# Attention on pairs of heads: wide turnings, scores in two row halves, values stationary, weights divided before the product

## The chip, the cores and the metric
One core of one Trainium2 chip. The metric is the device time of one execution in microseconds (us). All data are fp32; a product written in fp32 is issued on TensorE as two passes, and the large projections are split by hand into a high and a low part in fp32r.

## The reference, cut to what matters
Two layers, each a token mixer of three branches and a mixture of experts, over 128 context tokens (stream 0) and 128 latent tokens (stream 1). The change is in branch A, attention with 8 heads of 64 columns:

```
q, k, v = heads of proj columns; scale = 64 ** -0.5
context:  p = softmax(q k^T * scale);                 o = p v
latent:   q, k = axial_rope(q), axial_rope(k)
          s = [q k^T * scale + bias + window mask , q k_ctx^T * scale]
          p = softmax(s);                             o = p[:, :128] v + p[:, 128:] v_ctx
y_att = all heads' o side by side (128 x 512)
merged = gate0 * (y_att @ w_branch[0]) + gate1 * (y_ssm @ w_branch[1]) + gate2 * (y_gm @ w_branch[2])
```

## The kernel before, in words
The program is written out by hand for the five engines, and each runs its instructions in the order in which they stand; semaphores join them. In the mixer every weight piece (`PIECES`, 1 MB each) is loaded by SyncE's queue into one of four slots, its high part `wh` is made by ScalarE (`convert_to`, L1550) and its low part `wl` by VectorE (L1859), in three rotating parts; `ahead(key)` makes all pieces up to two behind `key`. TensorE then makes three groups of products for a piece. GpSimd's queue loads the rows for the modulation (`adaw`), sixteen slices in a layer, in two buffers.

The attention stage has four units in the order (stream s, head group g) = (0,0), (0,1), (1,0), (1,1), four heads each. TensorE's order in a unit: turn q and k of the unit (`turn4`, at s=1 also the cached keys `kctx`), a filler piece (`fill(FILL[3 * i])`), a modulation slice (`accumulate`), the scores, a second filler, two slices, turn S (`pw`, at s=1 also `pc`), a third filler, a slice, the product with v (at s=1 also with `vctx`) into bank `o`. In unit (1,0) it also turns `dtrow` and the modulation row `ada_row` ahead of the scores. After the four units it turns the rows of the branch, `branch_rows(l, 0, q)`, and after one more filler makes the branch's product.

VectorE's order in a unit: copy the turned q, k (and cached keys) to `qT`, `kT`, `cTk`; convert ahead; at i=2 the `dt` rows (`dtx`) and the modulation; read the scores: maximum and subtraction (s=0), or bias, window, copy, maximum, subtraction (s=1); after unit (0,1)'s scores the convolution of two blocks (`convolve`, `filled(3)`); convert ahead; then wait for `prob` and make the row sums of S (L2247) and their reciprocal (L2249); convert ahead; and last read bank `o`, multiplied by the reciprocal, into q. ScalarE makes the exponential of S (L1691, `prob`), copies the turned S to `pT` (L1698), and makes the activations of the fillers.

Banks 5, 6 and 7 are given out in turn to the small products (`odd` in `make_plan`); `bank_free` and `bank_emptied` wait until the last user of the bank has read it. `keep_busy` issues products whose result nobody reads.

## Time and profile before
| what | us |
|---|---|
| median of 3 runs | 1217.45 (1212.9 to 1221.46) |
| the profiled execution, its own time | 1216.07 |
| its span, first to last instruction | 1214.3 |
| TensorE busy | 1136.5 (94%) |
| VectorE busy | 634.9 (52%) |
| ScalarE busy | 442.4 (36%) |

The span is what the trace covers; the execution's own time has 1.8 us more around it. In the trace the attention stage of layer 0 lies from 78 to 181 us, that of layer 1 from 660 to 769 us. A busy share is a mean over the whole program; what counts for the change is, in these stretches, which engine is waited for at each hand-over.

### The profile page before, as it was taken

The page shows a single profiled execution, that of the slowest core. Times are in us where ns is not written, and L with a number is a line of the kernel's source. Part 1 is how long each engine was busy: PE and PEld are TensorE (multiplying, and loading weights), DVE is VectorE, ACT ScalarE, POOL GpSimd, SP SyncE. Part 2 cuts the span into 40 slices and gives each one's busy share as a digit, 9 for nine tenths or more (in the row PEclk, how much of TensorE's full clock was granted, in tenths as well). Part 3 has the DMA queues.
Part 4 walks back from the last instruction along what each step waited for, and adds up shares of the span by engine and source line. Part 5 has one row for each costly group of instructions (what it writes and reads, how often), then busy time and mean ns, then how long its engine had stood idle before and what let it go on. Part 6 is the DMA issues. An engine that isn't in the chain of part 4 may idle for free.

```text
span 1214.3 us, 18618 instructions
## 1 busy us (share of the span) xinstructions
PE 1136.5 (94%) x7288; PEld 787.3 (65%) x7288; DVE 634.9 (52%) x1298; ACT 442.4 (36%) x742; POOL 67.0 (6%) x113
## 2 busy tenths in 40 slices
PE   4999999999989999999979999999998989999994
PEld 0777777887766556666557776878776656666652
DVE  0645667788554533332278374679865453333224
ACT  0634553554332222222263344635533222222222
POOL 0401000101000000000020000010000000000000
PEclk8899999999999999999989989999998999999997
DMA  9997864546999999999667866556476999999960
GB/s 352 303 330 265 302 243 161 175 147 223 381 410 410 408 409 409 409 408 398 223 183 237 307 246 243 174 172 217 144 275 251 374 406 386 407 398 404 401 235 36
DMA packets 107981, 360.06 MB, mean 297 GB/s; under 512 B 9220, under 2 KB 12768, under 8 KB 99696
## 3 DMA queue, kind: packets, MB, share of 16 engines
q1 hardware_dynamic: 97392, 301.41, 66.0%
q0 software_dynamic: 10496, 57.39, 13.6%
q8 instruction: 61, 1.00, 0.3%
q14 instruction: 32, 0.26, 0.1%
HBM read 356.06 MB, written 3.74 MB: 296 GB/s over the span
## 4 chain that ended last, share of the span: by engine, by line
PE 68%; DVE 14%; DMA 5%; ACT 5%; issue 4%; DVEq 3%; ACTq 1%; SPq 0%
PE bank L920 63%; PE bank L923 5%; DVE wl L1859 3%; ACT wh L1550 2%; DMA adaw<-in_w_ada 2%; DMA first<-in_w_ada 2%; DMA raw<-in_w_in 1%; DVE merged L1859 1%; DVEq L2206 1%; DVE tmp L1859 1%; DVE tmp L2190 1%; DVE seg L2330 1%; DVE xbc L2125 0%; DVE xbc L2122 0%; DVE ygl L1859 0%
## 5 line engine op out<-in xcount | busy, mean ns | idle before, releaser
L1859 DVE TENSOR_TENSOR wl<-raw,wh 128x2048 fp32r<-128x2048 f32 (+1 forms) x76 | 169.1, 2236 | 61.5 <-ACT wh L1550 60.2
L1550 ACT ACTIVATE wh<-raw 128x2048 fp32r<-128x2048 f32 (+1 forms) x76 | 142.2, 1873 | 74.3 <-PE bank L920 53.4
L920 PE MATMUL bank<-wh,hTh 128*128 128x512 f32 x448 | 127.1, 406 | 0.4 <-ACT merged L1572 0.4
L920 PE MATMUL bank<-raw,xg 128*64 128x256 f32 x1088 | 123.3, 379 | 2.7 <-issue 2.7
L920 PE MATMUL bank<-wh,hTl 128*128 128x512 f32 x448 | 121.6, 393 | 0.0
L920 PE MATMUL bank<-wl,hTh 128*128 128x512 f32 x448 | 120.8, 392 | 0.0
L920 PE MATMUL bank<-wide,xg 128*64 128x256 f32 x1024 | 115.9, 379 | 0.0
L920 PEld LDWEIGHTS bank<-raw,xg 128*64 128x64 f32 x1088 | 78.4, 137 | 55.5 <-issue 21.6
L920 PEld LDWEIGHTS bank<-wide,xg 128*64 128x64 f32 x1024 | 73.6, 137 | 50.6 <-issue 18.3
L1859 DVE TENSOR_TENSOR ygl<-bank,ygh 128x512 fp32r<-128x512 f32 x66 | 45.6, 691 | 109.9 <-ACT ygh L1810 109.9
L920 PEld LDWEIGHTS bank<-wh,hTl 128*128 128x128 f32 x448 | 85.1, 190 | 19.0 <-DVE hTl L1859 0.4
L2555 DVE SCALAR_TENSOR_TENSOR hid<-bank,gg,sil 128x128 f32<-128x128 f32 x66 | 23.1, 350 | 141.7 <-ACT sil L1801 141.1
L920 PEld LDWEIGHTS bank<-wl,hTh 128*128 128x128 f32 x448 | 84.7, 189 | 18.3
L920 PEld LDWEIGHTS bank<-wh,hTh 128*128 128x128 f32 x448 | 82.7, 192 | 18.4 <-issue 2.7
L1801 ACT ACTIVATE sil<-bank 128x128 f32<-128x128 f32 x66 | 18.3, 278 | 186.9 <-PE bank L920 186.9
L2477 DVE TENSOR_SCALAR selT<-bank 128x256 fp32r<-128x256 f32 x66 | 28.0, 424 | 90.9 <-ACTq L1790 90.7
L1810 ACT ACTIVATE ygh<-bank 128x512 fp32r<-128x512 f32 x66 | 39.5, 598 | 88.9 <-PE bank L920 88.9
L920 PE MATMUL bank<-wide,hidT 128*64 128x512 f32 x272 | 65.9, 605 | 1.0 <-ACT hidT L1803 1.0
L920 PE MATMUL bank<-selb,x2h 128*128 128x256 f32 (+1 forms) x288 | 61.4, 304 | 2.8 <-DVE selb L2457 2.8
L920 PE MATMUL bank<-ygh,selT 64*128 64x512 f32 x264 | 59.0, 443 | 3.3 <-DVE ygl L1859 3.3
L920 PE MATMUL bank<-raw,hidT 128*64 128x512 f32 x256 | 62.0, 605 | 0.0
L1783 ACT ACTIVATE xg<-bank 128x512 f32<-128x512 f32 (+1 forms) x72 | 39.9, 562 | 45.3 <-PE bank L920 45.3
(307 smaller groups left out, 1634.4 us busy)
## 6 DMA issues: line engine op xcount, KB each, us to landing
raw<-in_moe_w SPq DMA_DIRECT2D x136, 512.0 KB, 8.3
wide<-in_moe_w SPq DMA_DIRECT2D x128, 512.0 KB, 8.7
raw<-in_w_in SPq DMA_DIRECT2D x52, 1024.0 KB, 7.0
wide<-in_moe_w SPq DMA_DIRECT2D x34, 1024.0 KB, 9.1
adaw<-in_w_ada POOLq DMA_DIRECT2D x32, 1024.0 KB, 6.9
raw<-in_moe_w SPq DMA_DIRECT2D x32, 1024.0 KB, 9.0
raw<-in_w_branch SPq DMA_DIRECT2D x12, 1024.0 KB, 5.3
raw<-in_w_ada SPq DMA_DIRECT2D x8, 1024.0 KB, 9.8
```

The source lines that it names most:

```text
L920: return behind(nc.tensor.matmul(*args, **kw))
L923: return behind(nc.tensor.transpose(*args))
L1550: A_(wh[c][:, 0:n], raw[:, r, 0:n], ACT.Copy).then_inc(part_high[c], 1)
L1783: A_(xg[b % 2][:, 2 * p:2 * p + 2, 0:n], bank[from_bank][:, :].rearrange("p (c n) -> p c n", c=2)[:, :, 0:n], ACT.Copy).then_inc(xg_ready, 1)
L1801: A_(sil[:, :], bank[UP_BANK][:, 0:P], ACT.Silu).then_inc(sil_done, run.step(k, MAIN - 1))
L1810: A_(ygh[:, :], bank[DOWN_BANK][:, :], ACT.Copy).then_inc(y_high, run.step(k, MAIN - 1))
L1859: return V.tensor_tensor(o, a, b, op)
L2190: return V.scalar_tensor_tensor(out=out, in0=gates_[:, s, hs], scalar=1.0, in1=t[:, :], op0=ALU.add, op1=ALU.mult)
L2206: drain()
L2330: ins = V.tensor_scalar(seg[:, n % 2, i, :], decay[n % 2][:, i, :], acs[:, s, 8 * r + h:8 * r + h + 1], 0.0, ALU.subtract, ALU.min)
L2477: V.tensor_scalar(selT[k % 2][:, :, :], bank[SELECT_BANK][:, 0:256].rearrange("p (s t) -> p s t", s=2), 0.0, None, ALU.is_gt).then_inc(sel ...
L2555: V.scalar_tensor_tensor(out=hid[:, :], in0=bank[UP_BANK][:, P:2 * P], scalar=gg[:, k % 2:k % 2 + 1], in1=sil[:, :], op0=ALU.mult, op1=ALU ...
```

## The change: what it does
- q and k of two heads are turned in one step, 128 columns wide: two turnings for q and two for k land in one bank, and one copy takes them to `qkT`, where an even head has partitions 0 to 63 and the odd one 64 to 127. The cached keys are turned in two steps.
- The scores of even heads use the upper 64 rows of the array and go to bank `sa`, those of odd heads the lower 64 rows and bank `sb`. At s=1 each bank holds both window and cached scores. VectorE reads the scores in two instructions, one for each bank. Both banks are asked for before the first score.
- VectorE multiplies S by the reciprocal of its row sums, right behind the reciprocal, and signals `normed`. TensorE waits for `normed` in place of `prob` before it turns S.
- In the values product v is stationary (64 columns) and the turned probabilities move, so a head's result lies in a half of the partitions and comes out turned. ScalarE takes each unit's bank `o` to `yT0h` as the high part and VectorE makes the low part `yT0l`; they lie where q and k were, so VectorE waits once in a layer until keys and values are stored. The turning of the branch's rows and the reads that belonged to it are gone.
- The rows of the branch's weights are read as `(c p)` in place of `(p c)`, the counts of `turned_high` go from 10 to 12 in a layer, and the banks' rotation is a new one.

```diff
@@ -192,22 +192,19 @@
         for g in range(2):
-            odd(f"qT{s}{g}"), odd(f"kT{s}{g}")
+            odd(f"qk{s}{g}")
             if s:
                 odd(f"cT{g}")
             if s and g == 0:
                 odd("dt")
                 odd("adaT1")
-            odd(f"sw{s}{g}")
-            if s:
-                odd(f"sc{g}")
+            odd(f"sa{s}{g}"), odd(f"sb{s}{g}")
             odd(f"pw{s}{g}")
             if s:
                 odd(f"pc{g}")
             odd(f"o{s}{g}")
     odd("adaT2")
     sides(4, 5, 6, 7)
-    turned(0)
     branch(0)
@@ -388,13 +385,15 @@
             ("xg0", [P, DC, BATCH * SEATS], F32, 0), ("xg1", [P, DC, BATCH * SEATS], F32, 8))
-        (q, k, v, uTh, uTl, gate1, z, u, gv, gate, merged,
+        (q, k, v, yT0h, yT0l, uTh, uTl, gate1, z, u, gv, gate, merged,
          first0, first1, first2, first3, adaw0, adaw1, x2h, x2l, ygh, ygl, hid, sil, weights, hidT, selb0, selb1,
          selg0, selg1, selT0, selT1, cum0, cum1, before_, one_of, product_, posx, which) = region(
             "mixer_rows", 40,
             ("q", [P, 2, NW], F32, 0),
             ("k", [P, 2, NW], F32, 4),
             ("v", [P, 2, NW], F32, 8),
+            ("yT0h", [P, 2, BC, P], F32R, 0),
+            ("yT0l", [P, 2, BC, P], F32R, 4),
             ("uTh", [P, BC, 2 * P], F32R, 0),
@@ -430,9 +429,9 @@
             ("which", [P, 8], F32, 35.5))
-        qT, kT, cTk, S, pT, yTh, yTl, W, eb, ctS, decay0, cbm, decay1, late3, lnrow = region(
+        qkT, cTk, S, pT, yTh, yTl, W, eb, ctS, decay0, cbm, decay1, late3, lnrow = region(
             "turned", 14,
-            ("qT", [HD, 4, P], F32, 0), ("kT", [HD, 4, P], F32, 2), ("cTk", [HD, 4, P], F32, 4),
+            ("qkT", [P, 2, 2, P], F32, 0), ("cTk", [P, 2, P], F32, 2),
             ("S", [P, 4, 2 * P], F32, 6),
...
@@ -1089,13 +1091,14 @@
                         t = bank_free(pe, l, f"br{b}{n}{s}")
-                        y_high, y_low = [p[:, :, s * P:(s + 1) * P] for p in rows_T[b]]
+                        y_high, y_low = [p[:, :, s * P:(s + 1) * P] if b else p[:, s] for p in rows_T[b]]
                         if n == 0:
-                            pe.wait_ge(turned_high, 10 * l + 2 * ORDER.index(b) + s + 1)
+                            pe.wait_ge(turned_high, 12 * l + (2 + 2 * ORDER.index(b) + s + 1 if b else 2 * s + 2))
                         for c in range(BC):
                             add(t[:, :], y_high[:, c, :], w[:, c, :], start=c == 0)
                         if n == 0:
-                            bank_emptied(pe, l, f"yT{b}{s}")
+                            for name in ([f"yT{b}{s}"] if b else [f"o{s}{g}" for g in range(2)]):
+                                bank_emptied(pe, l, name)
                         for c in range(BC):
@@ -1157,11 +1160,12 @@
                 for i, (s, g) in enumerate(UNITS):
-                    heads = range(4 * g, 4 * g + 4)
-                    turn4(l, f"qT{s}{g}", [q[:, s, h * HD:(h + 1) * HD] for h in heads], width=HD)
-                    turn4(l, f"kT{s}{g}", [k[:, s, h * HD:(h + 1) * HD] for h in heads], width=HD)
+                    def pairs(rows):
+                        return [rows[:, h * HD:(h + 2) * HD] for h in (4 * g, 4 * g + 2)]
+
+                    turn4(l, f"qk{s}{g}", pairs(q[:, s, :]) + pairs(k[:, s, :]))
                     if s:
-                        turn4(l, f"cT{g}", [kctx[:, h, :] for h in heads], width=HD)
+                        turn4(l, f"cT{g}", pairs(kctx[:, :, :].rearrange("t h d -> t (h d)")))
                     fill(FILL[3 * i])
@@ -1169,19 +1173,21 @@
                         turn_mod(l, 1, "adaT1")
-                    bank_emptied(pe, l, f"qT{s}{g}")
-                    bank_emptied(pe, l, f"kT{s}{g}")
+                    bank_emptied(pe, l, f"qk{s}{g}")
                     if s:
                         bank_emptied(pe, l, f"cT{g}")
-                    for name, keys in [(f"sw{s}{g}", kT)] + ([(f"sc{g}", cTk)] if s else []):
-                        t = bank_free(pe, l, name)
-                        for h in range(4):
-                            ins = mm(t[:, h * P:(h + 1) * P], qT[:, h, :], keys[:, h, :], start=True, stop=True)
-                        fills(ins, name)
+                    both = [bank_free(pe, l, f"s{a}{s}{g}") for a in "ab"]
+                    for n, keys in enumerate([qkT[:, 1]] + ([cTk] if s else [])):
+                        for j in range(2):
+                            for t, rows in zip(both, (slice(0, HD), slice(HD, 2 * HD))):
+                                ins = mm(t[:, (2 * n + j) * P:(2 * n + j + 1) * P], qkT[rows, 0, j, :], keys[rows, j, :],
+                                         start=True, stop=True)
+                                if n == s and j == 1:
+                                    fills(ins, f"s{'ba'[t is both[0]]}{s}{g}")
                     fill(FILL[3 * i + 1])
                     for n in range(1, 3):
                         accumulate(l, f"ada{pair}", ("ada", l, pair, c + n))
-                    pe.wait_ge(prob, l * 4 + i + 1)
+                    pe.wait_ge(normed, l * 4 + i + 1)
                     turn4(l, f"pw{s}{g}", [S[:, h, 0:P] for h in range(4)])
@@ -1189,16 +1195,16 @@
                     t = bank_free(pe, l, f"o{s}{g}")
-                    for h in range(4):
-                        hh = 4 * g + h
-                        ins = mm(t[:, h * HD:(h + 1) * HD], pT[:, 0, h, :], v[:, s, hh * HD:(hh + 1) * HD],
-                                 start=True, stop=not s)
-                        if s:
-                            ins = mm(t[:, h * HD:(h + 1) * HD], pT[:, 1, h, :], vctx[:, hh, :], start=False, stop=True)
+                    for j in range(2):
+                        for n in range(1 + s):
+                            for r in range(2):
+                                h = 2 * j + r
+                                hh = 4 * g + h
+                                rows = vctx[:, hh, :] if n else v[:, s, hh * HD:(hh + 1) * HD]
+                                ins = mm(t[r * HD:(r + 1) * HD, j * P:(j + 1) * P], rows, pT[:, n, h, :], start=n == 0, stop=n == s)
                     fills(ins, f"o{s}{g}")
                 fill(("gate", 0, 1, 0))
                 turn_mod(l, 2, "adaT2")
-                branch_rows(l, 0, q)
                 fill(("gate", 0, 1, 1))
...
@@ -1686,7 +1692,8 @@
                     else:
-                        bank_emptied(act, l, f"sw{s}{g}")
+                        bank_emptied(act, l, f"sa{s}{g}")
+                        bank_emptied(act, l, f"sb{s}{g}")
                     w = 2 * P if s else P
@@ -1698,10 +1705,11 @@
                     ahead(FILL[3 * i + 2])
+                    t = bank_full(act, l, f"o{s}{g}")
+                    A_(yT0h[:, s, 2 * g:2 * g + 2, :], t[:, 0:2 * P].rearrange("p (c t) -> p c t", c=2), ACT.Copy).then_inc(turned_high, 1)
                     filled(3 * i + 2)
                 ahead(("gate", 0, 1, 0))
                 take_row(l, 2, "ada2")
-                branch_turned(0)
                 ahead(("gate", 0, 1, 1))
...
@@ -2210,16 +2218,20 @@
                 for i, (s, g) in enumerate(UNITS):
-                    for dst, name in [(qT, f"qT{s}{g}"), (kT, f"kT{s}{g}")] + ([(cTk, f"cT{g}")] if s else []):
-                        t = bank_full(dve, l, name)
-                        frees(V.tensor_copy(dst[:, :, :], t[0:HD, :].rearrange("p (h t) -> p h t", h=4)), name)
+                    t = bank_full(dve, l, f"qk{s}{g}")
+                    frees(V.tensor_copy(qkT[:, :, :, :], t[:, :].rearrange("p (w j t) -> p w j t", w=2, j=2)), f"qk{s}{g}")
+                    if s:
+                        t = bank_full(dve, l, f"cT{g}")
+                        frees(V.tensor_copy(cTk[:, :, :], t[:, 0:2 * P].rearrange("p (j t) -> p j t", j=2)), f"cT{g}")
                     ahead(FILL[3 * i])
                     if i == 2:
                         step_in()
                         modulation(l, 1, "adaT1")
                     w = P
-                    t = bank_full(dve, l, f"sw{s}{g}")
-                    t3 = t[:, :].rearrange("t (h k) -> t h k", h=4)
+
+                    def scores(r, n):
+                        return bank_full(dve, l, f"s{'ab'[r]}{s}{g}")[:, 2 * n * P:2 * (n + 1) * P].rearrange("t (j k) -> t j k", j=2)
+
                     if i:
@@ -2229,18 +2241,21 @@
                         drain()
-                        frees(tt(S[:, :, 0:P], t3, S[:, :, P:2 * P], ALU.add), f"sw{s}{g}")
+                        for r in range(2):
+                            tt(S[:, r:4:2, 0:P], scores(r, 0), S[:, r:4:2, P:2 * P], ALU.add)
                         drain()
-                        t = bank_full(dve, l, f"sc{g}")
-                        frees(V.tensor_copy(S[:, :, P:2 * P], t[:, :].rearrange("t (h k) -> t h k", h=4)), f"sc{g}")
+                        for r in range(2):
+                            frees(V.tensor_copy(S[:, r:4:2, P:2 * P], scores(r, 1)), f"s{'ab'[r]}{s}{g}")
                         drain()
                         V.tensor_reduce(small[:, 20:24], S[:, :, :], X, ALU.max)
                         drain()
                         tt(S[:, :, :], S[:, :, :], bc(small[:, 20:24], 2, w), ALU.subtract).then_inc(smax, 1)
                     else:
-                        V.tensor_reduce(small[:, 20:24], t3, X, ALU.max)
+                        for r in range(2):
+                            V.tensor_reduce(small[:, 20 + r:24:2], scores(r, 0), X, ALU.max)
                         drain()
-                        frees(tt(S[:, :, 0:P], t3, bc(small[:, 20:24], 2, w), ALU.subtract), f"sw{s}{g}")
+                        for r in range(2):
+                            frees(tt(S[:, r:4:2, 0:P], scores(r, 0), bc(small[:, 20 + r:24:2], 2, P), ALU.subtract), f"s{'ab'[r]}{s}{g}")
                     filled(3 * i)
@@ -2248,17 +2263,18 @@
                     drain()
+                    tt(S[:, :, 0:w], S[:, :, 0:w], bc(small[:, 28:32], 2, w), ALU.mult).then_inc(normed, 1)
                     filled(3 * i + 1)
                     ahead(FILL[3 * i + 2])
-                    t = bank_full(dve, l, f"o{s}{g}")
-                    frees(tt(q[:, s, g * 256:(g + 1) * 256].rearrange("t (h d) -> t h d", h=4),
-                             t[:, 0:256].rearrange("t (h d) -> t h d", h=4), bc(small[:, 28:32], 2, HD), ALU.mult), f"o{s}{g}")
-                    if i == 3:
-                        drain().then_inc(y_ready[0], 1)
+                    if i == 0:
+                        dve.wait_ge(kv_stored, l + 1)
+                    dve.wait_ge(turned_high, 12 * l + i + 1)
+                    t = bank[USE[l][f"o{s}{g}"][0]]
+                    frees(tt(yT0l[:, s, 2 * g:2 * g + 2, :], t[:, 0:2 * P].rearrange("p (c t) -> p c t", c=2),
+                             yT0h[:, s, 2 * g:2 * g + 2, :].bitcast(F32), ALU.subtract), f"o{s}{g}")
                     filled(3 * i + 2)
                 ahead(("gate", 0, 1, 0))
                 modulation(l, 2, "adaT2")
-                branch_turned(0)
                 ahead(("gate", 0, 1, 1))
...
```

On VectorE, at the end of unit (0,1), stands before: the sums of S, the reciprocal, the conversion, and the read of bank `o` (which goes to `q`).

```order
L1859 TENSOR_TENSOR wl_52<-raw,wh_49 128x2048
L2247 TENSOR_REDUCE small<-S 128x4
L2249 RECIPROCAL small<-small 128x4
L1859 TENSOR_TENSOR wl_53<-raw,wh_50 128x2048
L1859 TENSOR_TENSOR q<-bank,small 128x256
L2132 COPY dtrow<-bank 16x256
```

And now, at the same place:

```order
L1867 TENSOR_TENSOR wl_52<-raw,wh_49 128x2048
L2262 TENSOR_REDUCE small<-S 128x4
L2264 RECIPROCAL small<-small 128x4
L1867 TENSOR_TENSOR S<-S,small 128x4x128
L1867 TENSOR_TENSOR wl_53<-raw,wh_50 128x2048
L1867 TENSOR_TENSOR yT0l<-bank,yT0h 128x256
L2140 COPY dtrow<-bank 16x256
```

A multiplication of S has come behind the reciprocal, and the read of bank `o` stands where it stood, with `yT0h` as its second operand.

On TensorE, unit (1,0), from the last passes of the first filler to the scores, before, with the engine's waits left out (`wl_52` is the low part of the filler's weights, `adaw_88` a modulation slice):

```order
L920 MATMUL bank<-wl_52,hTh 128x512 x4
L920 MATMUL bank<-adaw_88,cT 32x512 x4
L923 MATMUL bank<-cst,dtrow 128x16 x2
L920 MATMUL bank<-cst,ada_row 128x2x4 x4
L920 MATMUL bank<-kT,qT 128x128 x4
L920 MATMUL bank<-cTk,qT 128x128 x4
```

And now:

```order
L922 MATMUL bank<-wl_52,hTh 128x512 x4
L922 MATMUL bank<-adaw_90,cT 32x512 x4
L925 MATMUL bank<-cst,dtrow 128x16 x2
L922 MATMUL bank<-cst,ada_row 128x2x4 x4
L922 MATMUL bank<-qkT 128x128 x4
L922 MATMUL bank<-cTk,qkT 128x128 x4
```

The order is the same; what has moved is the bank requests. Before, the second group of scores alone used the bank of the `dt` rows; now the first score waits for it too.

## Rows read from the trace of the kernel before

**Rows 1.** The page, busy us by engine, share of the span, instructions

```profile
PE 1136.5 (94%) x7288; PEld 787.3 (65%) x7288; DVE 634.9 (52%) x1298; ACT 442.4 (36%) x742; POOL 67.0 (6%) x113
```

**Rows 2.** Waits of TensorE: us in total, times, longest us

```profile
PE bank L920 <- DMA adaw<-in_w_ada: 3.6, 3, 1.8
```

**Rows 3.** Timeline, TensorE, unit (0,0) of layer 0: start us, length us, what

```profile
78.30 0.60 PE L923 MATMUL bank<-cst,q 128*64 128x128 f32 x4 [2.33 <-ACTq L1609]
...
79.09 1.18 PE L920 MATMUL bank<-wh,hTh 128*128 128x512 f32 x4
...
85.74 1.16 PE L920 MATMUL bank<-kT,qT 64*128 64x128 f32 x8
86.82 1.21 PE L920 MATMUL bank<-wh,hTh 128*128 128x512 f32 x4
...
94.38 0.66 PE L923 MATMUL bank<-cst,S 128*128 128x128 f32 x4
...
102.39 1.10 PE L920 MATMUL bank<-v,pT 128*128 128x64 f32 x8
103.34 0.60 PE L923 MATMUL bank<-cst,q 128*64 128x128 f32 x4
```

**Rows 4.** Timeline, TensorE, later units of layer 0, unit (1,0) of layer 1

```profile
118.40 0.66 PE L923 MATMUL bank<-cst,S 128*128 128x128 f32 x4
...
134.34 1.16 PE L920 MATMUL bank<-kT,qT 64*128 64x128 f32 x8
...
144.38 1.09 PE L923 MATMUL bank<-cst,S 128*128 128x128 f32 x8
...
162.08 1.16 PE L920 MATMUL bank<-kT,qT 64*128 64x128 f32 x8
...
171.62 1.09 PE L923 MATMUL bank<-cst,S 128*128 128x128 f32 x8
...
730.65 1.09 PE L923 MATMUL bank<-cst,S 128*128 128x128 f32 x8
```

**Rows 5.** Timeline, VectorE, the same units

```profile
94.13 0.18 DVE L2249 RECIPROCAL small<-small 128x4 f32<-128x4 f32 x1
...
122.82 0.18 DVE L2249 RECIPROCAL small<-small 128x4 f32<-128x4 f32 x1
...
135.53 0.18 DVE L1859 TENSOR_TENSOR dtx<-bank,hrow 128x32 f32<-128x32 f32 x1
...
148.09 0.18 DVE L2249 RECIPROCAL small<-small 128x4 f32<-128x4 f32 x1
...
164.04 0.69 DVE L1859 TENSOR_TENSOR S<-bank,S 128x512 f32<-128x512 f32 x1
...
174.81 0.18 DVE L2249 RECIPROCAL small<-small 128x4 f32<-128x4 f32 x1
...
731.20 0.18 DVE L2249 RECIPROCAL small<-small 128x4 f32<-128x4 f32 x1
```

**Rows 6.** Timeline, TensorE, products in row halves and column halves in the scan

```profile
210.55 0.53 PE L920 MATMUL bank<-xbc 64*128 64x128 f32 x4
211.01 0.66 PE L923 MATMUL bank<-cst,xbc 128*128 128x128 f32 x4
...
212.72 0.44 PE L920 MATMUL bank<-xbc,cst 128*64 128x128 f32 x4
213.08 0.50 PE L920 MATMUL bank<-wh,hTh 128*128 128x512 f32 x1
```

**Rows 7.** Instructions on the tile S: ns min/median/max, starts, forms

```profile
L1859 DVE TENSOR_TENSOR S<-bank,small x4: 690/692/692, 87.7 to 695.8; 128x512 f32<-128x512 f32 x4
...
L1859 DVE TENSOR_TENSOR S<-S,small x4: 1225/1226/1227, 140.2 to 754.6; 128x1024 f32<-128x1024 f32 x4
```

**Rows 8.** Longest stand of TensorE late in the program; window: us, busy, clock, DMA, GB/s

```profile
921.66 2.34 PE L920 MATMUL bank<-chosen,cst 128*128 128x32 f32 x10 [4.40 <-DVEq L2434]
...
921.60:927.60 6.00, 5.60 (x20) 0.51 0.80 320
```

More of the change, by code:

```diff
@@ L180, in turned @@
         for s in range(2):
-            odd(f"yT{b}{s}") if b == 0 else plan.append((f"yT{b}{s}", (6, 4)[b - 1] + s))
+            plan.append((f"yT{b}{s}", (6, 4)[b - 1] + s))
     def branch(b):
@@ L445, in hybrid_backbone @@
             ("lnrow", [P, 2, D], F32, 0))
-        rows_T = [(yTh, yTl), (yTh, yTl), (uTh, uTl)]
+        rows_T = [(yT0h, yT0l), (yTh, yTl), (uTh, uTl)]
         xg, selb, selg, selT = (xg0, xg1), (selb0, selb1), (selg0, selg1), (selT0, selT1)
@@ L524, in hybrid_backbone @@
         pT_ready = sem("pT_ready")
-        y_ready = [sem(f"y_ready{b}") for b in range(3)]
+        y_ready = {b: sem(f"y_ready{b}") for b in (1, 2)}
+        normed = sem("normed")
         turned_high = sem("turned_high")
@@ L666, in source @@
                     n = piece[2]
-                    return lay(A["w_branch"], l)[piece[1]].rearrange("(p c) n -> p c n", c=BC)[:, :, n * 512:(n + 1) * 512]
+                    rows = lay(A["w_branch"], l)[piece[1]]
+                    rows = rows.rearrange("(p c) n -> p c n", c=BC) if piece[1] else rows.rearrange("(c p) n -> p c n", c=BC)
+                    return rows[:, :, n * 512:(n + 1) * 512]
                 if kind == "wo":
@@ L1295, in output @@
                             w = high_of(l, ("wo", i), 1024)
-                            pe.wait_ge(turned_high, 10 * l + 7 + 2 * s + i // 2)
+                            pe.wait_ge(turned_high, 12 * l + 9 + 2 * s + i // 2)
                             for h in range(2):
@@ L1960, in turned @@
                     t = bank[USE[l][name][0]][:, :].rearrange("p (c t) -> p c t", c=4)
-                    dve.wait_ge(turned_high, l * 10 + b + 1)
+                    dve.wait_ge(turned_high, l * 12 + b + 1)
                     if scale is None:
@@ L1969, in branch_turned @@
                         cols_ = slice(s * P, (s + 1) * P)
-                        turned(2 * ORDER.index(b) + s, f"yT{b}{s}", rows_T[b][0][:, :, cols_], rows_T[b][1][:, :, cols_])
+                        turned(2 + 2 * ORDER.index(b) + s, f"yT{b}{s}", rows_T[b][0][:, :, cols_], rows_T[b][1][:, :, cols_])
                 def residual(out, n):
@@ L2379, in _ @@
                         part = (slice(None), slice(4 * h, 4 * h + 4), slice(s * P, (s + 1) * P))
-                        turned(6 + 2 * s + h, f"mT{s}{h}", hTh[part], hTl[part], 0.5)
+                        turned(8 + 2 * s + h, f"mT{s}{h}", hTh[part], hTl[part], 0.5)
                 ahead(("wo", 3))
```

## The prediction
> **What bounds the kernel now.** The page first: the engine table says that TensorE is busy for 94% of the span [rows 1], so where it is busy only less of its work helps, and where it waits only an earlier release does. Then I laid TensorE's timeline beside VectorE's over the attention stage of layer 0 (78 to 181 us); layer 1 repeats it from 660 to 769 us. The stage has four units, (stream s, head group g). In each TensorE turns q and k, projects one filler piece, does the scores, another filler and two slices of the modulation row, turns the probabilities, and after a third filler and a slice makes the values product. In the list of waits TensorE hardly waits here: the largest entry is 3.6 us for modulation weights in three waits [rows 2]. So every pass that goes is a gain, as long as nothing else becomes late. What can become late is in VectorE's rows: set the start of its RECIPROCAL over the row sums against the start of TensorE's turning of S, unit by unit. It starts at 94.13, 122.82, 148.09 and 174.81 us [rows 5]; TensorE turns S at 94.38, 118.40, 144.38 and 171.62 [rows 3, 4]. In three of four units the reciprocal is 3 to 4 us later than the turning. That costs nothing now, since TensorE waits only for the exponential and the sum is used at the end of the unit.
>
> **What is removed from TensorE.** All but the turnings of q come as two passes to one product.
> (a) Turning q and k: eight turnings take 0.79 us (78.30 to 79.09 [rows 3]). Four wider ones replace them; TensorE turns 128 columns at the same pace, so half, 0.37 to 0.40 us, goes in each of four units, and 0.2 us more for the cached keys in the two units with s=1.
> (b) Scores: eight passes over 64 rows take 1.08 us (85.74 to 86.82 [rows 3]). Whether two row halves run abreast is shown by products that the scan already does that way, each half into its own bank: four passes from 210.55 to 211.01, 0.46 us [rows 6]. A further pass adds 0.12 us, the pace of the eight value passes, which take 0.95 us [rows 3]. So s=0: 0.46 + 2 x 0.12 = 0.70, a saving of 0.38; s=1 has twice as many: some 2.0 now against 1.18, a saving of 0.8.
> (c) Values: eight passes, 0.95 us (102.39 to 103.34 [rows 3]). Two column halves: four passes, 0.36 us (212.72 to 213.08 [rows 6]). So s=0: 0.60, saving 0.35; s=1: 1.08 against some 1.9, saving 0.8.
> (d) The eight turnings of the branch's rows after the stage: 0.8 us by the 0.79 for eight above [rows 3].
> Sum per layer: (a) 1.9, (b) 2.4, (c) 2.3, (d) 0.8: 7.4 us, 15 us for both, **if nothing waits**.
> In (b) and (c) the array changes how it is divided between operations. The Trainium skill, TensorEngine Tiling (Array Packing), Tiling Modes, Key Properties, says that changing the mode drains the engine, which speaks against small divided groups between whole-array fillers. The 0.46 and 0.36 us [rows 6] stand between whole-array work and hold any such cost already; by the page's "up to 2x" without it the scores of s=0 would take 0.54 and the sum would be some 1.4 us less in all.
>
> **The wait that is added.** The division moves from the product's rows to S itself, and TensorE now waits for `normed` in place of `prob`. Ahead of it on VectorE's queue stand, after the score reads: in unit (0,1) twelve convolution steps and a 2048-wide conversion, in the s=1 units a conversion that itself waits for ScalarE's; then the sum and the reciprocal, then the new multiplication. When can TensorE turn S? At the reciprocal's start plus a fixed part: the reciprocal with its drain 0.25; the multiplication, by the subtraction of the same shape, 0.69 us at s=0 and 1.23 at s=1 [rows 7]; the hand-over 0.05; and two reads of scores that are cut in halves, each a second instruction over the same elements, which lies between nothing and the 0.18 us that the reciprocal of four columns takes [rows 5], taken at 0.08, so 0.16. That is 1.15 at s=0 and 1.70 at s=1. It comes earlier by what the scores come earlier after the last unit's end: (a)+(b).
> How much later than before is the turning of S, each counted from the end of the unit ahead:
> - (0,0): 94.13 - 94.38 + 1.15 - 0.75 = +0.15.
> - (0,1): 122.82 - 118.40 + 1.15 - 0.75 = +4.8 [rows 4, 5].
> - (1,0): 148.09 - 144.38 + 1.70 = +5.4, and the savings don't count: the chain starts at the read of the dt rows (135.53 [rows 5]), which hangs on the third convolution, and that now stands behind the low part of the values, which waits for ScalarE's high part: +0.35. Both score banks are asked for before the first score, and one of them is freed by that read, so TensorE, there at 134.34 already, also waits some 2 us ahead of the scores. Sum +5.8.
> - (1,1): 174.81 - 171.62 + 1.70 = +4.9. The chain starts with the bias sum, which now needs no scores, so it runs from the scores' end: begin 162.08 - 0.57 [rows 4], + 1.18 + 0.1 = 162.8 against 164.04 [rows 5], -1.25. Sum +3.65.
> Layer 0: +14.4. In layer 1 the first, second and fourth are the same; in unit (1,0) TensorE was late itself, 730.65 against a reciprocal at 731.20 [rows 4, 5]: 0.55 + 1.70 + 0.35 = +2.6. Layer 1: +11.2. **Together +25.6.**
> Against it what is saved behind each turning of S: (c) 2.3 and (d) 0.8 in each layer, 6.2; and the 3.6 us of modulation waits [rows 2], whose loads are issued before the new wait and land during it, 3.3. **Net +16 us at full clock.**
>
> **The clock.** TensorE would stand for the lateness plus what it saved ahead: 5.6, 5.4 and about 5 us, three times in each layer. The nearest row is a stand of 4.40 us before 921.66; in the 6 us after it the granted clock is 0.51, half speed, 1.2 in place of 2.4 GHz [rows 8]. Half of 6 us is 3.0, the upper bound; nothing, should the clock stay up, the lower. A part of the slow stretch can fall into the stand itself, so I take 2.3 us for each of six: **+14**. What follows each stand is a filler that nothing hides, so all of it is on the path.
> Work costed at nothing: the four smaller ScalarE reads of the values and VectorE's four low parts take the place of two wide ones each and of the old division by row; they are hidden by the filler that follows, as the copies are today. VectorE's wait for the stored keys costs nothing, since those stores stand in GpSimd's queue ahead of modulation loads that TensorE has used by then. The branch weights are read in rows of the same length.
>
> **The sum.** The profiled execution took 1216.07 us (span 1214.3), 1.4 under the median: 1216.1 + 16 + 14 = **1246**.
>
> **Rivals.**
> - The wait isn't there (faster): if `normed` came within the 7.6 us that filler and modulation slices give TensorE after the scores (86.82 to 94.38 [rows 3]), all 15 us count, and some waits go: about 1202. It decides at a reciprocal that starts 1.2 (s=0) or 1.7 us (s=1) ahead of TensorE. [rows 5] show it 0.25 ahead at the best and 3 to 4 behind otherwise; for it only that VectorE's conversion might slide, but it is in order. 4%.
> - The clock stays up, or falls at one or two stands only: 1216 + 16, to 1216 + 16 + 5: 1232 to 1237. For it: the stands are bounded on both sides by dense work, unlike the one of [rows 8], which has tiny products after it. 24%.
> - The stands are shorter than reckoned, since VectorE's chain runs from the scores' end and scores, bank waits or the cover of convolutions come sooner: +4 to +12: 1220 to 1229. 8%.
> - The halves do not run abreast in this form (operands from one tile): (b) and (c) give nothing; (b) delays the chain by 1.5 us in a layer, (c) adds 2.3: 8 us more, 1254; or the waits ahead of the (1,0) scores pull the clock down too. Against it [rows 6]. 9%.
> The Trainium skill, same page, Performance Considerations, PSUM Bottleneck, has it that dividing the array speeds TensorE but not the reading of its banks. As a mechanism here it is the forecast's: [rows 5] say that the reader of the scores, not the scores, sets the time. By it alone, with no division moved, the gain of (b) would be hidden and the rest kept, 1216 - 10 = 1206, which is in the first rival's chance.
>
> **How the numbers follow.** Forecast, 55%: 1240 to 1254, 1246 likeliest. The range takes in the shorter stands' upper half and most of the case of 1254: 1226 to 1257. No change from slower needs 12 us, 1%, about what a measurement of this kernel can tell: slower by more than that is the forecast, the clock case and the last, 88%; same 8%, faster 4%.
>
> **What would show it.** Right: TensorE waits of about 5 us ahead of its turning of S, ended by VectorE's S multiplication, three in each layer, and one of about 2 us ahead of the scores of (1,0), ended by dtx; granted clock 0.5 behind them; score groups of 0.6 to 0.7 us at s=0; the modulation waits gone. Wrong: no idle time there, or a multiplication that starts before TensorE comes; stands without a fall of the clock; score passes one behind the other; or a new wait in the branch product, for the low parts.

## The result and the profile after

The changed kernel takes 1243.86 us (median of 4 runs, 1241.99 to 1247.19) against 1216.8 for the kernel before (median of 4 by then): ratio 1.0225, 95% interval 1.0194 to 1.0257. It is slower by 2.2%. The forecast was 1246.

The profiled execution is the longest of the four, 1247.19 us, span 1245.4; that is 31.1 us more than the span of before, where the medians are 27 apart. The page, busy us by engine, answers to [rows 1]:

```profile
PE 1139.0 (91%) x7232; PEld 783.9 (63%) x7232; DVE 635.3 (51%) x1310; ACT 443.4 (36%) x746; POOL 66.9 (5%) x113
```

TensorE has 56 passes fewer and is busy 2.5 us more: busy time counts passes at half clock at their length, and passes that run abreast only once, so it tells nothing of the gain. The time in which it does nothing has grown from 77.8 to 106.4 us (span less busy time): 94% has become 91%.

TensorE's waits, us in total, times, longest, answer to [rows 2]:

```profile
PE bank L925 <- DVE S L1867: 30.9, 8, 5.6
...
PE bank L922 <- DVE dtx L1867: 4.5, 2, 2.2
...
PE bank L922 <- DMA adaw<-in_w_ada: 0.4, 1, 0.4
```

The first row is the wait that was added: eight waits, one for each unit, ended by VectorE's multiplication of S. That it is as long as the whole loss is chance: what the layout saves and what the clock costs stand against each other beside it. The dt rows' wait is the one ahead of the scores of (1,0). The modulation waits, 3.6 before, are 0.4.

The timeline of TensorE in layer 0, start, length, what, and in brackets the idle time before, answers to [rows 3, 4]:

```profile
84.47 0.71 PE L922 MATMUL bank<-qkT 64*128 64x128 f32 x8
85.12 1.21 PE L922 MATMUL bank<-wh,hTh 128*128 128x512 f32 x4
...
94.88 0.66 PE L925 MATMUL bank<-cst,S 128*128 128x128 f32 x4 [1.97 <-DVE S L1867]
...
103.72 0.66 PE L922 MATMUL bank<-pT,v 128*64 128x128 f32 x8
104.31 0.44 PE L925 MATMUL bank<-cst,q 128*128 128x128 f32 x2
...
124.17 1.11 PE L925 MATMUL bank<-cst,S 128*128 128x128 f32 x4 [5.54 <-DVE S L1867]
...
143.92 1.23 PE L922 MATMUL bank<-qkT 64*128 64x128 f32 x8 [2.23 <-DVE dtx L1867]
...
158.43 1.09 PE L925 MATMUL bank<-cst,S 128*128 128x128 f32 x8 [2.99 <-DVE S L1867]
...
187.81 1.97 PE L925 MATMUL bank<-cst,S 128*128 128x128 f32 x8 [4.89 <-DVE S L1867]
```

Eight score passes take 84.47 to 85.12, 0.65 us, where they took 1.08; eight value passes 0.59 where they took 0.95. So the layout does what it should. And ahead of each turning of S stands what it costs.

VectorE in unit (0,1), start, length, what, answers to [rows 5]:

```profile
112.46 0.76 DVE L2255 TENSOR_REDUCE small<-bank 128x2 f32<-128x256 f32 x2 [5.32 <-PE bank L922]
...
120.22 2.28 DVE L1867 TENSOR_TENSOR wl<-raw,wh 128x2048 fp32r<-128x2048 f32 x1
122.42 0.68 DVE L2262 TENSOR_REDUCE small<-S 128x4 f32<-128x512 f32 x1
123.17 0.18 DVE L2264 RECIPROCAL small<-small 128x4 f32<-128x4 f32 x1
123.42 0.69 DVE L1867 TENSOR_TENSOR S<-S,small 128x512 f32<-128x512 f32 x1
```

The multiplication is 0.69 us long and ends 11.6 us after the first read of the scores: what is late is not the work but its place behind twelve convolution steps and a conversion. TensorE resumes at 124.17, at once.

ScalarE in unit (0,0), which had no such row between scores and exponential before:

```profile
86.89 1.28 ACT L1698 ACT_TABLE_LOAD   x1 [7.49 <-DVE S L1867]
88.19 0.63 ACT L1698 ACTIVATE S<-S 128x512 f32<-128x512 f32 x1
```

The granted clock (columns: window, us, TensorE busy, clock, DMA share, GB/s), answers to [rows 8]:

```profile
95.50:98.90 3.40, 3.40 (x18) 0.50 1.01 419
122.80:129.60 6.80, 5.43 (x26) 0.50 0.78 290
143.30:150.10 6.80, 6.18 (x26) 0.50 0.70 269
158.40:165.20 6.80, 6.77 (x36) 1.00 0.90 363
187.70:191.10 3.40, 3.29 (x12) 0.50 0.58 225
225.20:228.60 3.40, 3.40 (x11) 0.50 0.30 112
```

Half clock (1.2 GHz) behind the stands of 1.97, 5.54 and 4.89 us and around the wait for the dt rows; full clock behind the stand of 2.99. The last row lies outside the attention stage. In layer 1 the clock is at half for 6.8 us from 720.1, 740.6 and 785.0, and for 3.4 us behind the stand of 3.45 us in (1,0):

```profile
757.70:761.10 3.40, 3.40 (x10) 0.50 1.01 410
```

Where the 31.1 us are, from the starts of the units (first turning of q) and of the turnings of S in the two timelines, in us; the last interval of a layer goes to the turning of `ada_row` behind the stage:

| unit | start to turning of S, before | after | later | turning of S to the unit's end, before | after | later |
|---|---|---|---|---|---|---|
| layer 0 (0,0) | 16.08 | 17.47 | +1.39 | 8.96 | 9.43 | +0.47 |
| (0,1) | 15.06 | 19.86 | +4.80 | 6.85 | 8.82 | +1.97 |
| (1,0) | 19.13 | 25.44 | +6.31 | 9.33 | 8.51 | -0.82 |
| (1,1) | 17.91 | 20.87 | +2.96 | 14.86 | 15.65 | +0.79 |
| layer 1 (0,0) | 16.10 | 17.39 | +1.29 | 9.52 | 7.91 | -1.61 |
| (0,1) | 15.07 | 19.87 | +4.80 | 6.72 | 8.51 | +1.79 |
| (1,0) | 22.78 | 25.72 | +2.94 | 11.23 | 10.11 | -1.12 |
| (1,1) | 17.39 | 20.87 | +3.48 | 14.86 | 16.17 | +1.31 |
| sum | | | +28.0 | | | +2.8 |

30.8 of 31.1 us lie in the two attention stages.

### The profile page after: what moved, and what is told of

The parts are those of the page before. It is cut to its first block, busy times and chain, and to the rows that moved or that the text cites. A ratio compares the mean times of both kernels' runs of the same rounds, so it can differ in the third digit from the quotient of the medians.

```text
span 1245.4 us, 18504 instructions
## 1 busy us (share of the span) xinstructions
PE 1139.0 (91%) x7232; PEld 783.9 (63%) x7232; DVE 635.3 (51%) x1310; ACT 443.4 (36%) x746; POOL 66.9 (5%) x113
## 4 chain that ended last, share of the span: by engine, by line
PE 64%; DVE 16%; ACT 6%; issue 4%; DVEq 4%; DMA 4%; ACTq 1%; SPq 0%; POOL 0%; POOLq 0%
PE bank L922 60%; PE bank L925 4%; DVE wl L1867 4%; ACT wh L1556 3%; DMA first<-in_w_ada 2%; DMA raw<-in_w_in 1%; DVE S L1867 1%; DVE merged L1867 1%; DVEq L2214 1%; DVEq L2263 1%; DVE seg L2346 1%; DVE tmp L2198 1%; DVE tmp L1867 1%; DMA decay<-decay_rows 1%; DVE xbc L2133 0%
## 5 line engine op out<-in xcount | busy, mean ns | idle before, releaser
L922 PEld LDWEIGHTS bank<-wl,hTh 128*128 128x128 f32 x448 | 85.1, 190 | 18.4
```

The costliest lines, as they stand in the source:

```text
L922: return behind(nc.tensor.matmul(*args, **kw))
```

## The experiments

Each ratio is to the kernel before, run on the same chip, with its 95% interval.

**1. No division.** On the changed kernel:

```diff
-                    pe.wait_ge(normed, l * 4 + i + 1)
+                    pe.wait_ge(prob, l * 4 + i + 1)
...
-                    tt(S[:, :, 0:w], S[:, :, 0:w], bc(small[:, 28:32], 2, w), ALU.mult).then_inc(normed, 1)
```

> The changed kernel without the multiplication of S by the reciprocal, and TensorE waits for prob again (S goes into the product undivided; nothing else is left out). Theory (the moved division makes TensorE late and its clock fall): the 31 us of waits ahead of the turning of S are gone, and with them the half-clock stretches behind them. What stays is the saving of 15 us, less about 2 us in each layer for the wait on the dt rows ahead of the scores of unit (1,0): 1203 to 1208. Rival (the new layout itself is slow: array modes, halved reads, the high and low parts of each unit in line): it stays above 1225.

Measured: 1201.0 us, ratio 0.9852 (0.9815 to 0.9889). No wait for S is in the list any more. The first theory holds, and the time is 2 us below its range: without the division the layout is worth some 18 us. In TensorE's waits of this kernel the one for the dt rows is there as foreseen:

```profile
PE bank L921 <- DVE dtx L1866: 4.5, 2, 2.2
```

**2. The division alone.** On the kernel before:

```diff
-                    pe.wait_ge(prob, l * 4 + i + 1)
+                    pe.wait_ge(normed, l * 4 + i + 1)
...
                     V.reciprocal(small[:, 28:32], small[:, 24:28])
                     drain()
+                    tt(S[:, :, 0:w], S[:, :, 0:w], bc(small[:, 28:32], 2, w), ALU.mult).then_inc(normed, 1)
...
-                    frees(tt(q[:, s, g * 256:(g + 1) * 256].rearrange("t (h d) -> t h d", h=4),
-                             t[:, 0:256].rearrange("t (h d) -> t h d", h=4), bc(small[:, 28:32], 2, HD), ALU.mult), f"o{s}{g}")
+                    frees(V.tensor_copy(q[:, s, g * 256:(g + 1) * 256], t[:, 0:256]), f"o{s}{g}")
```

> The kernel before, in which only the division moves: S is multiplied by the reciprocal and TensorE waits for that; the read of bank o becomes a plain copy. Theory: lateness of the turning of S 0.7, 5.4, 5.2 and 4.7 us in layer 0 and 0.7, 5.4, 2.1 and 4.7 in layer 1, together 29, less 3 of modulation waits, plus 10 to 14 for the clock: 1250 to 1256, so slower than the changed kernel. Rival (most of the loss is from the other parts): under 1235.

Measured: 1254.13, ratio 1.0299 (1.0258 to 1.034), within the 1250 to 1256 expected. This one part of the change, without the new layout, gives the loss, and more of it. TensorE's waits of this kernel:

```profile
PE bank L924 <- DVE S L1860: 32.0, 8, 5.7
```

**3. TensorE kept busy in the stands.** On the changed kernel; products with no reader go into the bank that the turning then overwrites:

```diff
+                    stay_busy(l, f"pw{s}{g}", (6, 22, 22, 20)[i])
                     pe.wait_ge(normed, l * 4 + i + 1)
```

> The changed kernel with products whose result nobody reads put on TensorE ahead of each wait for normed (6, 22, 22 and 20 of 128x512 bf16, about 1.3 and 4.8 us), into the bank that is turned into next. Theory of the clock: the chains stay as long, but the granted clock doesn't fall behind the waits, which gives back the half-clock work behind them, 9 to 12 us: 1232 to 1235. Rival (the clock costs nothing, since what runs at half clock is hidden by other engines): 1243 to 1245. If the products outlast a wait, it is slower by that.

Measured: 1240.97, ratio 1.0188 (1.0146 to 1.023), against 1.0225 for the changed kernel; the intervals overlap, so the traces must tell. The time lies between the 1232 to 1235 of the theory and the 1243 to 1245 of the rival. The timeline of this kernel, TensorE, unit (0,1) of layer 0:

```profile
119.55 4.92 PE L922 MATMUL bank<-cst 128*128 128x512 bf16 x22
125.15 0.66 PE L925 MATMUL bank<-cst,S 128*128 128x128 f32 x4 [0.68 <-DVE S L1875]
```

The granted clock behind that wait, same kernel and columns as above:

```profile
125.10:131.60 6.50, 6.45 (x57) 1.00 0.59 210
```

The clock stays at 1.00 and the unit takes 26.25 us in place of 28.68. Whole units, this kernel against the changed one, layer 0 and 1: (0,1) -2.4 and -2.1, (1,1) -1.5 and -2.1, together -8.2 us; (1,0) +0.4 and -0.5, (0,0) +0.1 and +0.4.

Counted only from the turning of S to the unit's end, the eight units take 85.1 us in sum in the changed kernel and 73.7 here, where none of it is at half clock. These 11.4 us are what the fallen clock costs behind the stands, and they lie in the 9 to 12 of the theory. What hides them is ahead of the turnings, which come 3.6 us later in sum. In (1,0) the 22 products outlast the wait (the turning starts without one), since TensorE comes late there anyhow; it comes 0.5 and 1.1 us later, and 0.5 in (0,0) of layer 1 in the same way. In (0,0) of layer 0, 3.4 us of half clock lie at the start of the unit (from 78.9), and its turning comes 1.6 us later.

**4. The division early in VectorE's queue.** On the changed kernel:

```diff
-                    filled(3 * i)
-                    ahead(FILL[3 * i + 1])
                     dve.wait_ge(prob, l * 4 + i + 1)
                     V.tensor_reduce(small[:, 24:28], S[:, :, 0:w], X, ALU.add)
...
                     tt(S[:, :, 0:w], S[:, :, 0:w], bc(small[:, 28:32], 2, w), ALU.mult).then_inc(normed, 1)
+                    filled(3 * i)
+                    ahead(FILL[3 * i + 1])
```

> The changed kernel with another order on VectorE: the wait for prob, the sums, the reciprocal and the multiplication come directly behind the subtraction, and convolution and conversion after them. Theory: VectorE reaches the division of s=0 within 5.5 us after the scores and that of s=1 within 8.4, against the 7.6 that TensorE needs, so the waits ahead of turning S shrink from 31 us to 3 to 5 and the clock stays up there; the work moved behind makes the third convolution and so the dt rows later, 3 to 4 us of wait in each layer ahead of the scores of unit (1,0). 1206 to 1216. Rival (the exponential, not the queue on VectorE, sets the division, or the moved work stalls the fillers): above 1230.

Measured: 1208.51, ratio 0.9906 (0.9877 to 0.9934), as expected. The same instructions in another order turn a loss of 2.2% into a gain of 0.9%. The waits of TensorE for S are one of 0.6 us. The convolutions' delay has come up where it was looked for, ahead of the scores of (1,0), with 4.5 us in each layer for 3 to 4 expected: most of it through ScalarE, which takes the modulation row only after the third convolution's activation. TensorE's waits of this kernel:

```profile
PE bank L922 <- ACT ada_row L1541: 6.3, 2, 3.2
...
PE bank L922 <- DVE dtx L1867: 2.7, 2, 1.7
...
PE bank L925 <- DVE S L1867: 0.6, 1, 0.6
```

**5. One wait ahead of the exponential.** On the changed kernel:

```diff
                     else:
-                        bank_emptied(act, l, f"sa{s}{g}")
                         bank_emptied(act, l, f"sb{s}{g}")
```

> The changed kernel, in which ScalarE waits ahead of the exponential of s=0 for bank sb alone (its read stands behind that of sa on VectorE's queue, so nothing is lost). Theory: with two waits the first was taken by the activation table's load, which so came behind the scores and added 1.28 us to the chain; with one wait the load runs ahead. Unit (0,0) gets 1.3 us earlier in each layer; in unit (0,1) nothing, since the convolutions on VectorE are longer than the exponential. 2 to 4 us less than the changed kernel: ratio to the kernel before 1.019 to 1.021. Rival (the load is free, as its idle time was there before): 1.022 to 1.023.

Measured: 1236.27, ratio 1.0172 (1.013 to 1.0214). It is lower than 1.0225 and than the 1.019 to 1.021 expected, but the intervals overlap; the mechanism is in the trace. The table's load runs ahead of the wait now (79.43, the exponential at 88.47), as in the kernel before (80.22 and 88.43). In layer 1 unit (0,0) takes 23.97 us in place of 25.30, its wait for S is 0.37 us in place of 1.57. In layer 0 the turning of S comes no earlier (17.76 us into the unit, 17.47 in the changed kernel), since 3.4 us of half clock lie at the unit's start here, from 78.7. So the load accounts for 2.6 us at most, 1.28 in each layer. The rest of the difference to the changed kernel is not explained by it, and the half-clock stretches lie elsewhere in this execution. ScalarE's timeline of this kernel, layer 0:

```profile
79.43 1.28 ACT L1697 ACT_TABLE_LOAD   x1
88.47 0.63 ACT L1697 ACTIVATE S<-S 128x512 f32<-128x512 f32 x1 [7.76 <-DVE S L1866]
```

**6. The halves one behind the other.** On the first experiment's kernel, the loops over halves outside:

```diff
-                    for n, keys in enumerate([qkT[:, 1]] + ([cTk] if s else [])):
-                        for j in range(2):
-                            for t, rows in zip(both, (slice(0, HD), slice(HD, 2 * HD))):
-                                ins = mm(...)
+                    for t, rows in zip(both, (slice(0, HD), slice(HD, 2 * HD))):
+                        for n, keys in enumerate([qkT[:, 1]] + ([cTk] if s else [])):
+                            for j in range(2):
+                                ins = mm(...)
...
-                    for j in range(2):
-                        for n in range(1 + s):
-                            for r in range(2):
+                    for r in range(2):
+                        for j in range(2):
+                            for n in range(1 + s):
```

> The kernel without the division (S undivided, as in the first experiment), in which all scores of the upper row half are issued and then all of the lower, and the values products by column half in the same way. Theory (neighbouring halves run abreast, ones in line can't): score groups of s=0 grow from 0.65 to 1.0 us, values of s=0 from 0.6 to 1.0, twice that at s=1, 3 to 4 us in a layer, part of it hidden behind the dt rows: 1206 to 1208 against 1201. Rival (the gain was from fewer and wider passes, not from running abreast): 1201.

Measured: 1207.05, ratio 0.9925 (0.99 to 0.9951) against 0.9852. The total came out as forecast and the reason did not. Groups of s=0 are as short as before, values from 99.74 to 100.34, 0.60 us, in this kernel's timeline of TensorE:

```profile
99.74 0.66 PE L921 MATMUL bank<-pT,v 128*64 128x128 f32 x8
100.34 0.44 PE L924 MATMUL bank<-cst,q 128*128 128x128 f32 x2
```

Four passes of one half and then four of the other still overlap. Only with eight and eight is there a part in line: the values of (1,1) take 177.41 to 178.92, 1.5 us. That is 1 us for both groups of such a unit, 4 us for the four of them. The two stages are 6.3 us longer in the traces than in the first experiment's kernel; most of the rest is the clock, at half for 6.8 us around the scores of (1,0) in each layer where it was 3.4. This kernel's window in layer 0:

```profile
132.50:139.30 6.80, 6.80 (x26) 0.50 0.57 212
```

So the order of issue was the wrong way to forbid running abreast.

**7. All passes in the same half.** On the first experiment's kernel:

```diff
-                                ins = mm(t[:, ...], qkT[rows, 0, j, :], keys[rows, j, :],
+                                ins = mm(t[:, ...], qkT[0:HD, 0, j, :], keys[0:HD, j, :],
...
-                        for n in range(1 + s):
-                            for r in range(2):
+                        for r in range(2):
+                            for n in range(1 + s):
...
-                                ins = mm(t[r * HD:(r + 1) * HD, j * P:(j + 1) * P], rows, pT[:, n, h, :], ...)
+                                ins = mm(t[0:HD, h * P:(h + 1) * P], rows, pT[:, n, h, :], ...)
```

> The kernel without the division (first experiment), in which all scores use the upper 64 rows of the array (those of odd heads are made from even heads' data) and all values products the left 64 columns, so that no two passes lie in different halves; counts, shapes and waits are the same. Theory: passes of one half can't run abreast, so score groups of s=0 grow from 0.65 to 1.1 us and values from 0.6 to 0.95, at s=1 by 0.8 to 0.9 each: 4.5 to 5 us in a layer, 9 to 10 in all: 1209 to 1212 against 1201. Rival (the saving is from the wider turnings alone): 1201 to 1203.

Measured: 1213.79, ratio 0.9968 (0.9936 to 1.0) against 0.9852: 14 us, where 9 to 10 were expected; the time is 2 us above the range. The timeline of this kernel, TensorE, layer 0:

```profile
83.98 1.16 PE L921 MATMUL bank<-qkT 64*128 64x128 f32 x8
85.07 1.21 PE L921 MATMUL bank<-wh,hTh 128*128 128x512 f32 x4
...
99.95 1.09 PE L921 MATMUL bank<-pT,v 128*64 128x128 f32 x8
100.97 0.44 PE L924 MATMUL bank<-cst,q 128*128 128x128 f32 x2
```

Scores of s=0 take 1.09 in place of 0.65 us, values 1.02 in place of 0.59. So the groups are shorter since passes run abreast; the wider turnings alone don't explain the gain. In the traces the two stages are 11.3 us longer, of which 3.4 us more of half clock around (1,0) in each layer are a part.

**8. The kernel before with an early division.** The second experiment's kernel with the order of the fourth:

```diff
-                    filled(3 * i)
-                    ahead(FILL[3 * i + 1])
                     dve.wait_ge(prob, l * 4 + i + 1)
...
                     tt(S[:, :, 0:w], S[:, :, 0:w], bc(small[:, 28:32], 2, w), ALU.mult).then_inc(normed, 1)
+                    filled(3 * i)
+                    ahead(FILL[3 * i + 1])
```

> The kernel before with the division moved to S (second experiment, 1254 us), and on VectorE in the early place: wait for prob, sums, reciprocal and multiplication directly behind the subtraction, then convolution and conversion. Theory (what costs is the place in VectorE's queue, not the multiplication): the 32 us of waits go to 2 to 5, and what the convolutions lose ahead of unit (1,0) is 4 to 6 us in a layer as in the fourth experiment: 1218 to 1228. Rival (the multiplication before the turning costs by itself): above 1240.

Measured: 1223.27, ratio 1.0044 (1.0019 to 1.0069), and 1.7 us of waits for S in all. So the multiplication before the turning costs 0.4% in the early place and 3.0% in the late one. Against the fourth experiment, which has the same order, the layout alone is worth 1.0044 against 0.9906.

**9. The version that follows.** The fourth and fifth together, and in unit (1,0): ScalarE takes `ada_row` and converts before the third convolution's activation; VectorE reads the dt rows and the modulation before its conversion, which goes between the subtraction and the sums.

```diff
                     if i == 2:
                         step_in()
                         modulation(l, 1, "adaT1")
+                    else:
+                        ahead(FILL[3 * i])
...
+                    if i == 2:
+                        ahead(FILL[3 * i])
                     dve.wait_ge(prob, l * 4 + i + 1)
...
                         take_row(l, 1, "ada1")
                     ahead(FILL[3 * i])
+                    if i == 2:
+                        filled(5)
...
-                    filled(3 * i + 2)
+                    if i != 1:
+                        filled(3 * i + 2)
```

> The changed kernel with the division ahead on VectorE (as in the fourth experiment), one wait ahead of the exponential, and unit (1,0) freed: ScalarE takes the modulation row before the third convolution's activation, and VectorE reads the dt rows and the modulation before its conversion, which goes between the subtraction and the sums. Theory: of the fourth experiment's time the waits of 3.2 us for the modulation row and 1.1 to 1.7 for the dt rows go in each layer, with the slow clock behind them, 8 to 12 us; a wait of about 1 to 2 us ahead of turning S of (1,0) may come: 1197 to 1202, ratio to the kernel before 0.981 to 0.986. Rival (another wait takes their place, since VectorE is full there): 1206 to 1209.

Measured: 1198.05, ratio 0.9845 (0.9807 to 0.9884): faster than the kernel before by 1.6% and than the changed one by 3.7%. It lies in the 1197 to 1202 expected. The largest of TensorE's waits that are left in the stages, in this kernel:

```profile
PE bank L925 <- DVE S L1869: 2.9, 3, 1.7
...
PE bank L922 <- DMA adaw<-in_w_ada: 2.4, 3, 1.6
```

## Why the prediction was right, point by point

- **The bound.** That TensorE's passes are the bound and VectorE's late reciprocal the danger: right, by experiments 1, 2, 4 and 8.
- **What is removed**, 7.4 us in a layer if nothing waits. In the trace the score group of s=0 saves 0.43 (0.38 foreseen) and the values 0.36 (0.35). That the halves run abreast, read off [rows 6], is shown by experiment 7.
- **The wait that is added.** Foreseen +25.6 us of lateness, measured +28.0, by unit in the table above. (0,1) is exact, +4.8 in both layers. (0,0) is off by 1.1 to 1.2 each, +1.39 and +1.29 for +0.15: I cut the score reads in two and priced them, but did not see that the second bank wait ahead of the exponential pushes the table's load behind the scores (experiment 5). In (0,1) the same load is hidden by the convolutions. (1,0) was +6.3 and +2.9 for +5.8 and +2.6; the wait ahead of its scores was 2.2 us in both layers for some 2 foreseen. (1,1) was +3.0 and +3.5 for +3.65.
- **The clock.** Foreseen +14 for six stands. What it cost behind them is the difference to the third experiment's kernel, from the turning of S to the unit's end, where that kernel has no half clock (and the first experiment's, again without one, has the same 74 us in sum): (0,1) 2.4 and 2.1, (1,1) 1.5 and 2.1, (1,0) 0.0 and 1.6, together 9.8 us. So this term was mis-sized by some 4 us, more than half of it in (1,0) of layer 0. There TensorE waited 2.2 us ahead of the scores and ran at half clock around them, so it reached the turning of S late and stood 2.99 us only, where 5.4 were foreseen, and the clock was at 1.00 behind it. In layer 1 the same unit had a stand of 3.45 us, and 3.4 us of half clock behind it. A seventh cost was not foreseen at all: 1.5 us behind the stand of 1.97 in (0,0) of layer 0. In all 11.4.
- **Behind the turning of S** the sum foreseen was -4.6 for the values, -3.3 for the modulation waits and +14 for the clock, +6.1; measured +2.8, which is -8.6 (82.3 before against 73.7 without half clock) and +11.4. The modulation waits went as forecast, 3.6 to 0.4.
- **Outside the stages** -1.6 was foreseen for the turnings of the branch's rows, measured +0.3. Those turnings are gone. In their place the trace has half-clock stretches that the one of before lacks, the one at 225.2 for instance, or 17.1 us from 945.4 where before had 6.8 from 920.7; whether they follow from the change or from chance no run here tells.
- **Sum.** 25.6 + 6.1 - 1.6 = 30 foreseen, 28.0 + 2.8 + 0.3 = 31 measured. That it fits to 1 us is in part luck: the lateness came out 2.4 us above (the table's load) and the part outside the stages 1.9, the part behind the turnings 3.3 below, most of it the clock.
- **The rivals.** The case without a fall of the clock (1232 to 1237) is ruled out by the half-clock rows and the 11.4 us. The one of halves that don't run abreast is ruled out by experiment 7; what it had beside that, a clock pulled down by the waits ahead of the (1,0) scores, did come, 6.8 us at half clock in each layer, of which the kernel before has 6.8 in layer 1 too (from 719.3). The one of shorter stands (1220 to 1229) was right on (1,0) and wrong on the time, since the turnings were later all the same. The fast case had its condition right: where the division comes in time, as in experiments 4 and 9, the savings count, 1208 and 1198 us. Of the signs of being wrong the wait for the low parts in the branch's product is not in TensorE's list.

The Trainium skill's PSUM Bottleneck (TensorEngine Tiling (Array Packing), Performance Considerations) agrees with the traces here in one point: VectorE's read of a bank group at s=0 went from one instruction of 0.69 us to two of 0.76 together, while the group's passes went from 1.08 to 0.65. But what was worth 43 us between experiment 1 and the changed kernel was not the reading of banks; it was an instruction that reads none.

## What to carry to other kernels

Before a result that was used late is asked for early, read when it is ready now, not how long it takes to make: the multiplication itself took 0.69 us where it was read, but it made TensorE late by 28.0 us over eight units, 3.5 us each. The reading that gave this is two columns of one table, the start of the producer and the start of the consumer-to-be in each unit. And when an operation moves onto the chain, everything else on its engine's queue has to be asked again for its place; here the early place alone was worth 35 us (experiment 4), and 46 with the other moves of experiment 9, more than the layout's 18.

## What was not expected of the hardware

- An activation table's load can come behind a wait of the activation that it belongs to. With one wait it ran ahead of it, at 79.43 with the exponential at 88.47. With two it started at 86.89, 0.07 us after VectorE's second read of the scores ended, with the exponential right behind it, and put 1.28 us on the chain.
- Passes in different halves of the array overlap though four of one half are issued before four of the other: 0.60 us for the group, as when they take turns. With eight and eight it is 1.5 us against 1.0.
- A stand of 1.97 us in layer 0 (0,0) was followed by 3.4 us at a granted clock of 0.50 from 95.5 on, one of 2.99 ahead of 158.43 by none: the length of a stand alone does not tell whether the clock falls.
